# Loading attention's first operands during the recurrence, in the buffer that the projections leave

## What is computed

```python
for window, dil in ((128, 1), (512, 4), (2048, 16)):      # attention, 8 heads x 64
    # positions of equal residue mod dil form a band of window // dil + 1 keys,
    # swept in blocks of 128 queries: own block and the one before
    s = einsum('...qhd,...khd->...hqk', q, k) * ATTN_SCALE + bias
    p = exp(s - max(s)); out, lse = p @ v / sum(p), max(s) + log(sum(p))
# the three outs are weighed by softmax(lse)
S_t = diag(f_t) S_{t-1} + (1 - f_t) i_t^T;  o_t = S_t^T q_t   # recurrence, 4 heads
```

## Time and profile before

| | us |
|---|---|
| median of 3 runs | 1754.37 |
| profiled execution, its own time | 1760.19 |
| its span | 1758.4 |
| TensorE busy | 1570.9 |
| VectorE busy | 806.8 |
| ScalarE busy | 475.8 |
| GpSimd busy | 353.6 |

### The profile page before, as it was taken

One profiled execution on the slowest core, in us unless ns is written; L12 is line 12 of the kernel. 1 busy time (PEld: TensorE's weight loads), 2 busy tenths in 40 slices (PEclk: granted clock), 3 DMA queues, 4 the chain that ended last, 5 costly groups with the idle time before them and its releaser, 6 DMA issues. The chain is left out here.

```text
span 1758.4 us, 26175 instructions
## 1 busy us (share of the span) xinstructions
PE 1570.9 (89%) x9834; PEld 1411.0 (80%) x9834; DVE 806.8 (46%) x2031; ACT 475.8 (27%) x1350; POOL 353.6 (20%) x269
## 2 busy tenths in 40 slices
PE   8999999979899989999799995499989995399987
PEld 7999999966687767777599995498979895277775
DVE  6111200023232142111179883175737574699995
ACT  5111111121001132222201221165646565212210
POOL 1333200001500010000000002538482932011111
PEclk9999999989899989999959997697969798599999
DMA  9999992338748598757201886928592814555541
GB/s 307 350 324 327 338 284 73 127 110 258 213 140 318 181 308 249 271 162 245 88 1 63 259 276 180 257 59 180 144 213 63 169 51 148 216 182 211 212 152 42
DMA packets 180895, 340.67 MB, mean 194 GB/s; under 512 B 16323, under 2 KB 116099, under 8 KB 173443
## 3 DMA queue, kind: packets, MB, share of 16 engines
q1 hardware_dynamic: 147100, 173.77, 31.0%
q10 hardware_dynamic: 21248, 108.93, 19.4%
q0 software_dynamic: 12432, 56.48, 12.1%
HBM read 263.40 MB, written 156.48 MB: 239 GB/s over the span
## 5 line engine op out<-in xcount | busy, mean ns | idle before, releaser
L254 PE MATMUL acc<-xhi,whi 128*128 128x424 f32 (+1 forms) x640 | 227.3, 355 | 8.5 <-DVE xlo L233 8.5
L743 PE MATMUL nacc<-nwhi,nxhi 128*128 128x512 f32 (+1 forms) x544 | 220.2, 405 | 9.2 <-DVE nwlo L492 9.2
L254 PE MATMUL acc<-xlo,whi 128*128 128x424 f32 (+1 forms) x640 | 227.0, 355 | 0.0
L254 PE MATMUL acc<-xhi,wlo 128*128 128x424 f32 (+1 forms) x640 | 226.9, 355 | 0.0
L1320 ACT ACTIVATE spare<-spare 128x256 f32<-128x256 f32 (+1 forms) x384 | 174.1, 454 | 165.0 <-DVE spare L1295 161.9
L743 PE MATMUL nacc<-nwlo,nxhi 128*128 128x512 f32 (+1 forms) x544 | 215.6, 396 | 0.0
L743 PE MATMUL nacc<-nwhi,nxlo 128*128 128x512 f32 (+1 forms) x544 | 215.2, 396 | 0.0
L1252 POOL CAST a_sorted<-a_plain 128x2048 fp32r<-128x2048 f32 x48 | 181.6, 3855 | 154.5 <-PE a_s_ps L1360 128.5
L1295 DVE CUSTOM_DVE_ANT_0 spare<-a_s_ps,a_bias 128x256 f32<-128x256 f32 (+1 forms) x384 | 125.3, 364 | 167.4 <-PE a_s_ps L1360 167.2
L1384 PE MATMUL a_o_ps<-a_v,a_probT 128*128 128x64 f32 x1200 | 170.3, 284 | 20.3 <-DMA a_v<-projN 20.0
L1384 PEld LDWEIGHTS a_o_ps<-a_v,a_probT 128*128 128x128 f32 x1200 | 164.4, 208 | 21.8 <-issue 21.0
(11 more groups left out here) (170 smaller groups left out, 2530.8 us busy)
## 6 DMA issues: line engine op xcount, KB each, us to landing
out_kwin_s<-in_cache_kT ACTq DMA_DIRECT2D x8, 2048.0 KB, 18.3
split_qk<-spare POOLq DMA_DIRECT2D x16, 1024.0 KB, 13.3
spare<-in_xT SPq DMA_DIRECT2D x32, 512.0 KB, 7.6
projN<-nstage SPq DMA_DIRECT2D x32, 512.0 KB, 5.9
qg<-in_cache_kT ACTq DMA_DIRECT2D x8, 2048.0 KB, 10.8
d_vlow<-in_cache_v ACTq DMA_DIRECT2D x8, 2048.0 KB
out_kwin_s<-in_cache_kT ACTq DMA_DIRECT2D x8, 2032.0 KB, 26.1
out_vwin_s<-in_cache_v ACTq DMA_DIRECT2D x8, 2032.0 KB, 16.9
```

The costliest lines, as they stand in the source:

```text
L254: mm = pe.matmul(acc[:, j, 0:n], w[:, u, k], x[:, k, c0:c0 + n], start=(k == 0 and a == 0), stop=(k == KD - 1 and a == 2))
L743: mm = pe.matmul(acc[0:m, n % 2], x[:, u, k, 0:m], w[:, k, g * H:(g + 1) * H], start=(k == 0 and b == 0), stop=(k == KD - 1 and b == 2))
```

## The change

- `spare` lives on the other side of SBUF and only until the projections end. In its room stand, from the start of the recurrence, `plain` of both heads, `ident` and the bias rows of group 0. `stage` and `prob` get buffers of their own, `v` becomes two buffers and so does `bias`.
- POOL issues both `load_pair`s of group 0 in `hgrn_prompt`, right after its memset of `at`; SP issues the identity and `load_bias` of group 0 there, after `load(1)`.
- At the start of attention SP issues `load_values(0)`, the bias of group 1, `load_values(1)`; POOL goes straight to its wait and the sorts.
- `load_pair` loads whole rows: 6 transfers for x = 0 too, in every group. `FRONT` and `front_landed` are gone; TensorE waits for `pair_landed[x]` at the first unit of each head.

```diff
-    def sb(name, shape, dt=F32):
-        return ctx.enter_context(nc.sbuf_tensor(name, shape, dt))
+    def sb(name, shape, dt=F32, side="left"):
+        return ctx.enter_context(nc.sbuf_tensor(name, shape, dt, side=side))
...
+def load_pair(pool, split_qk, plain_x, g, x, landed):
+
+    hs = slice(x * DA, (x + 1) * DA)
+    for n, w, low, half in ((0, 0, 0, 0), (0, 0, 1, 1), (1, 1, 0, 0), (1, 1, 0, 1), (2, 1, 1, 0), (2, 1, 1, 1)):
+        pool.dma_start(plain_x[half * DA:(half + 1) * DA, n], split_qk[w * NG + g, low, hs]).then_inc(landed, 16)
+
+
+def load_bias(sp, rep_p, bias_u, g, landed):
+    L = HA * NC * LB
+    for x in range(2):
+        src = bass.AP(tensor=rep_p.tensor, offset=(2 * g + x) * NC * LB + P - 1, ap=[[L - 1, P], [LB, NC], [1, 2 * P]])
+        sp.dma_start(bias_u[:, x], src).then_inc(landed, 16)
+
+
+def hgrn_prompt(nc, projT, projN, o_b, state_out, first, win, copied, split_qk, rep_p, ident_d, keep):
...
                 load(0)
                 load(1)
+                sp.dma_start(keep["ident"][:], ident_d).then_inc(keep["const"], 16)
+                load_bias(sp, rep_p, keep["bias"][0], 0, keep["bias_landed"][0])
                 for s in range(NSEG):
...
                 nc.gpsimd.memset(at[:], 0.0).then_inc(zeroed, 1)
+                for x in range(2):
+                    load_pair(pool, split_qk, keep["plain"][x], 0, x, keep["pair_landed"][x])
...
-        plain = [sb(f"a_plain{x}", [P, 3, T], F32R) for x in range(2)]
-        ns, np_ = 2 * NBK * 2 * OW, 4 * 2 * 2 * P
-        stage = keep["spare"][:, 0:ns].rearrange("p (w b x e) -> p w b x e", w=2, b=NBK, x=2)
-        prob = keep["spare"][:, ns:ns + np_].rearrange("p (n y k) -> p n y k", n=4, y=2)
-        v = sb("a_v", [P, 2, NC, NBK, P])
-        bias = sb("a_bias", [P, 2, 2, NC, 2 * P])
+        plain, ident, bias = keep["plain"], keep["ident"], keep["bias"]
+        v = [sb("a_v0", [P, NC, NBK, P], side="right"), sb("a_v1", [P, NC, NBK, P])]
+        stage = sb("a_stage", [P, 2, NBK, 2, OW])
+        prob = sb("a_prob", [P, 4, 2, 2 * P])
         probT = sb("a_probT", [P, 3, 4, P])
-        ident = sb("a_ident", [P, P])
+        bias.append(sb("a_bias1", [P, 2, NC, 2 * P]))
         sorted_ = sb("a_sorted", [P, 2, 3, T], F32R)
         s_ps, t_ps, o_ps = ps("a_s_ps", [P, 3, 512]), ps("a_t_ps", [P, 3, 512]), ps("a_o_ps", [P, 2, 512])
...
-        FRONT = 4 * P
-
-        def load_part(pool, w, g, x, c0, c1, landed):
-
-            hs = slice(x * DA, (x + 1) * DA)
-            for n, low, half in ((0, 0, 0), (0, 1, 1)) if w == 0 else ((1, 0, 0), (1, 0, 1), (2, 1, 0), (2, 1, 1)):
-                pool.dma_start(plain[x][half * DA:(half + 1) * DA, n, c0:c1], split_qk[w * NG + g, low, hs, c0:c1]
-                              ).then_inc(landed, 16)
-
...
-                load_bias(0)
-                sp.dma_start(ident[:], ident_d).then_inc(const, 16)
                 load_values(0)
-                load_bias(1)
+                load_bias(sp, rep_p, bias[1], 1, bias_landed[1])
                 load_values(1)
...
-                def load_pair(g, x):
-                    if x == 0:
-                        load_part(pool, 0, g, 0, 0, FRONT, front_landed)
-                        load_part(pool, 1, g, 0, 0, FRONT, front_landed)
-                    for w in range(2):
-                        load_part(pool, w, g, x, 0 if x else FRONT, T, pair_landed[x])
-
                 def sort(g, c, x):
                     d = DILS[c]
                     if c == 1:
-                        if x == 0:
-                            pool.wait_ge(front_landed, 96 * (g + 1))
                         pool.wait_ge(pair_landed[x], 96 * (g + 1))
...
-                load_pair(0, 0)
-                load_pair(0, 1)
...
-                            load_pair(g + 1, x)
+                            load_pair(pool, split_qk, plain[x], g + 1, x, pair_landed[x])
...
-                                pe.wait_ge(pair_landed[1] if x else front_landed, 192 * i + 96 * (u + 1))
-                            if c == 0 and x == 0 and P * (b + 2) == FRONT + 2 * P:
-                                pe.wait_ge(pair_landed[0], 192 * i + 96 * (u + 1))
+                                pe.wait_ge(pair_landed[x], 192 * i + 96 * (u + 1))
...
+        keep = {"ost_free": [sem(f"h_ost_free{u}") for u in range(2)], "state_kept": sem("h_state_kept"), "const": sem("a_const"),
+                "pair_landed": [sem(f"a_pair_landed{x}") for x in range(2)], "bias_landed": [sem(f"a_bias_landed{u}") for u in range(2)]}
+        with ExitStack() as mid:
             with ExitStack() as ctx:
                 sb, _, _ = region(ctx, nc)
-                first["bounds"] = sb("bounds", [P, 4, HB])
-                first["lmask"], first["dmask"] = sb("lmask", [P, len(PLEVELS), CH // 2], I32), sb("dmask", [P, CH], I32)
-                first["ident"], first["qg"] = sb("ident3", [P, P]), sb("qg", [P, 4 * HB * SEG])
-                halves = first["qg"][:].rearrange("p (a u h t) -> p a u h t", a=2, u=2, h=HB)
-                first["q"], first["sg"] = halves[:, 0], halves[:, 1]
-                project_natural(nc, a, projT, projN, o["kwin_p"], o["vwin_p"], o["kwin_s"], o["vwin_s"], rep_p, rep_d, o_b,
-                                attn_s, o["hgrn_s"], spare, w_landed, x_landed, first)
-                hgrn_prompt(nc, projT, projN, o_b, o["hgrn_p"], first, win, copied, keep)
-            attention_prompt(nc, split_qk, projN, rep_p, a["ident"], partials, keep)
+                with ExitStack() as early:
+                    spare = region(early, nc)[0]("spare", [P, 2 * KD * XCOLS], side="right")
+                    project_transposed(nc, a["xT"], a["w_t"], projT, split_qk, win, copied, spare, a["w_n"], w_landed, x_landed)
+                    first["bounds"] = sb("bounds", [P, 4, HB])
+                    first["lmask"], first["dmask"] = sb("lmask", [P, len(PLEVELS), CH // 2], I32), sb("dmask", [P, CH], I32)
+                    first["ident"], first["qg"] = sb("ident3", [P, P]), sb("qg", [P, 4 * HB * SEG])
+                    halves = first["qg"][:].rearrange("p (a u h t) -> p a u h t", a=2, u=2, h=HB)
+                    first["q"], first["sg"] = halves[:, 0], halves[:, 1]
+                    project_natural(nc, a, projT, projN, o["kwin_p"], o["vwin_p"], o["kwin_s"], o["vwin_s"], rep_p, rep_d, o_b,
+                                    attn_s, o["hgrn_s"], spare, w_landed, x_landed, first)
+                right = region(mid, nc)[0]
+                keep["plain"] = [right(f"a_plain{x}", [P, 3, T], F32R, side="right") for x in range(2)]
+                keep["ident"], keep["bias"] = right("a_ident", [P, P], side="right"), [right("a_bias0", [P, 2, NC, 2 * P], side="right")]
+                hgrn_prompt(nc, projT, projN, o_b, o["hgrn_p"], first, win, copied, split_qk, rep_p, a["ident"], keep)
```

More of the change, by code:

```diff
@@ L855, in load_segment @@
     sp.dma_start(q[:, u], projT[8:12, :, t0:t0 + SEG].rearrange("h p t -> p h t")).then_inc(landed[u], 16)
-def hgrn_prompt(nc, projT, projN, o_b, state_out, first, win, copied, keep):
+def load_pair(pool, split_qk, plain_x, g, x, landed):
[8 more added lines that the diff above has]
+def hgrn_prompt(nc, projT, projN, o_b, state_out, first, win, copied, split_qk, rep_p, ident_d, keep):
     NG2 = HB // 2
@@ L1108, in _, with attention_prompt @@
                     read_out(NSEG - 1, c)
-def attention_prompt(nc, split_qk, projN, rep_p, ident_d, partials, keep):
+def attention_prompt(nc, split_qk, projN, rep_p, partials, keep):
     NBK = T // P
@@ L1163, in attention_prompt @@
         stage_free = [sem(f"a_stage_free{w}") for w in range(2)]
-        const, s_done, p_done, p_turn, e_done = (sem(f"a_{n}") for n in ("const", "s_done", "p_done", "p_turn", "e_done"))
+        s_done, p_done, p_turn, e_done = (sem(f"a_{n}") for n in ("s_done", "p_done", "p_turn", "e_done"))
         t_done, pt_done, pv_done, o_out = (sem(f"a_{n}") for n in ("t_done", "pt_done", "pv_done", "o_out"))
-        front_landed, sort_done = sem("a_front_landed"), sem("a_sort_done")
-        pair_landed = [sem(f"a_pair_landed{x}") for x in range(2)]
-        bias_landed = [sem(f"a_bias_landed{u}") for u in range(2)]
+        pair_landed, bias_landed, const = keep["pair_landed"], keep["bias_landed"], keep["const"]
+        sort_done = sem("a_sort_done")
         NLD = 6
-        FRONT = 4 * P
-        def load_part(pool, w, g, x, c0, c1, landed):
-            hs = slice(x * DA, (x + 1) * DA)
-            for n, low, half in ((0, 0, 0), (0, 1, 1)) if w == 0 else ((1, 0, 0), (1, 0, 1), (2, 1, 0), (2, 1, 1)):
-                pool.dma_start(plain[x][half * DA:(half + 1) * DA, n, c0:c1], split_qk[w * NG + g, low, hs, c0:c1]
-                              ).then_inc(landed, 16)
         with nc.Block() as block:
@@ L1183, in _ @@
                 sp.sem_inc(stage_free[1], 16)
[L1185 to L1191, removed]
                 def load_values(g):
@@ L1196, in load_values @@
```

(10 more changed lines are left out.)

2 lines of the change are left out of this document (1 added, 1 removed).

## The result

The changed kernel takes 1727.42 us (median of 4 runs, 1725.64 to 1729.23), against 1756.19 us (4 runs, 1753.92 to 1759.91) for the kernel before on the same chip: ratio 0.983, 95% interval [0.981, 0.986]. It is 28.8 us faster where 69 were forecast, and lies 18 us above the upper end of the range.

The account below looks back on a forecast made before the run. TensorE bounds attention through a 20.0 us wait for values (transfer rate at the start) and 12.4 us of sort waits that halve its clock. 31.9 + 9.2 + 22.2 + 5.7 = 69.0 us off 1754.4 gives 1685.4, said 1686; range 1678 to 1709.

Parts of the forecast that it names:

- Part 1: Start of attention: pair, bias and identity loads move into the recurrence, so the wait for the values ends 31.9 us earlier.
- the case in which the change does not do what it says: Start of attention: SP's slow issuing was its own, values still land near 1134; 1717 us, chance 0.05.
- the slowing weighed there: Recurrence: busy VectorE may lock out GpSimd's descriptor writing; even ten times slower issues, 60 us, would fit the slack.
- Part 2: Unit 40, groups 0 to 2: six issues fewer start sort(2, 1) 3.08 us earlier per group, 9.2 us in all.
- Part 3: Behind unit 40's 1.0 us wait: the clock holds, giving 22.2 us in units 40 to 47 and 5.7 us after.
- The row from the merge: Merge: TensorE waits 1.26 us before each tile's transposes at clock 1.00, taken as evidence that the clock holds.
- The 22.2 us of units 40 to 47: Groups 0 to 2: at full clock these eight units take 8.96 us instead of 16.38, three times.
- the 5.7 behind them: After unit 47: full clock gains 1.0 and 2.3 us at borders of groups 0 and 2, 2.4 at the loop's turn.
- The second case: Units 40 to 47: the clock still falls after 1 us waits, only 41.1 us are left; 1713 us, chance 0.18.
- Part 4: Unit 48: TensorE now waits for the whole next pair, which lands in time with 5 us to spare; costs nothing.
- three of 1 us: Unit 40, groups 0 to 2: TensorE still waits 1.0 us instead of 4.1 in each group.

Follow-up runs that it names:

- experiment 1: Changed kernel with x = 0 pair loads cut into 12 transfers again and the 512-column wait restored, early loads kept; 1725.53 us, ratio 0.982 to the kernel before.
- experiment 8: Kernel before with only SP's order at the start of attention changed: identity, values, then bias of group 0; no early load; 1760.96 us, ratio 1.002.
- experiment 2: Kernel before with only whole-row pair loads (6 transfers for x = 0) and no waits for `front_landed`; 1754.91 us, ratio 0.9987.
- experiment 3: Changed kernel with six identity products before TensorE's wait for the sort at unit 40, in all four groups; 1728.95 us, ratio 0.983 to the kernel before.
- 5: Changed kernel with identity products before unit 40's wait and the x = 1 load held until the c = 1 store has landed; 1716.29 us, ratio 0.977.
- 6: Changed kernel with SP issuing the pair loads of groups 1 to 3, x = 0 ahead of the c = 1 store, x = 1 behind it; 1702.11 us, ratio 0.969.
- experiment 7: Changed kernel without the pair loads of groups 1 to 3, which attend with group 0's queries and keys; 1687.82 us, ratio 0.960 to the kernel before.
- 9: Against the kernel whose later pair loads SP issues: x = 1 for group 2 loaded behind the c = 2 stores; 1698.76 us, ratio 0.967 to the kernel before.
- experiment 4: Changed kernel with POOL holding the x = 1 load until the c = 1 results' store has landed; 1720.59 us, ratio 0.978 to the kernel before.

## Why the prediction was wrong

**Part 1 was right.** 30.9 us instead of 31.9, with the values 1 us later than taken; experiment 1 gives it alone, 31.5 us by its ratio. That the start is bound by transfer rate and not by SP's order is what experiment 8 shows, so the case in which the change does not do what it says is out. The loads were issued in 6.18 us beside a busy VectorE, so the slowing weighed there did not occur. They ended at about 910 instead of 902, still deep in the empty stretch.

**Part 2 was right in its term** (8.8 us instead of 9.2), and worth little in the end: 2.3 us in experiment 2.

**Part 3 is the step that failed:** "I take it that the clock holds." It fell within two units of waits of 1.24, 1.19 and 1.19 us. The 22.2 us of units 40 to 47 became 3.3, and of the 5.7 behind them nothing came: the turn took 1.0 more. The row from the merge did not carry over. The runs agree on it: with 4.2 us of wait (1) and with 1.2 us (the changed kernel, 2) the clock falls, with the wait filled by products (3, 5) or not there (6, 7, 9) units 40 to 47 stay at 1.00. The length of the wait does not decide it alone, though. Of nine waits of 1.16 to 1.25 us at unit 40 (the changed kernel, 2 and 4) eight brought the clock down, and the one in group 1 of experiment 4 did not. At unit 56, the first of x = 1, waits of 3.15 us (5), 1.62 us (6) and 1.22 us (9) brought it down, and waits of 1.30 us (6), 1.27 and 2.35 us (9) did not. What else decides stays open, and neither place had a wait shorter than 1.16 us. So the forecast's rows could not settle the question either way.

The second case, with a chance of 0.18, was the right one on the clock. The section "HAM oscillation — how this bites in real kernels" of the Trainium skill's TensorE: Matmul & The Clock Gate page warns that waits between bursts of matmuls throttle the engine again and again. The traces agree with it for eight of the nine waits at unit 40, which are 1.2 us, and differ for the ninth.

**Part 4 left a resource out.** It asked only whether the next pair lands in time for unit 48, and it does. It did not ask what else must get through while 6.3 MB of loads are under way, with a DMA share of 1.0 to 1.26 from 1160 to 1185. Three things do, and each holds up TensorE once it arrives early enough: the c = 1 store, for which VectorE waits (4 takes that wait away); the operands of x = 1 (5 and 6); and whatever the "issue" gaps at the turn stand for. The first of those gaps is 2.13 us where the loads are over the earlier trace rows and 2.59 in the changed kernel, where they are nearly over; it is 8 to 9 where they are under way (3, 4, 5, 6), 3.2 without them (7) and 4.05 with one put off (9). The likely reading is the fetch of the new turn's instructions, which cross the same DMA engines. The packets of the instruction queues bear it out: in all eleven traces the last packet of queue 8 ahead of the warm-up ends 1.5 to 1.8 us before it (2.5 in experiment 2), and in 3, 4, 5 and 6 another ends about 1.3 us before the warm-up's second part. With the loads out of the way (7) the first such packet starts 0.4 us into the gap, in 6 it starts 4.7 us into it. Since the traces do not say whose instructions a packet carries, that the gap depends on the loads is shown, and that the fetch is what waits is strongly suggested.

The store is why the changed kernel is at 1727 and not at the second case's 1713: set against the profiled run of before the second case gives 1719.1, and 1729.2 were measured. Of the 10.1 between them the borders' waits are 9.3, the merge's 1.4, the turn 1.0 and what parts 1 and 2 fell short 1.4, less the 3.3 that units still at full speed won; 0.3 is left over. It is also why the forecast would have failed with a clock that held: experiment 3 had that clock, and took 1729 us. Only experiment 7, without the loads, reached 1688, two above the number predicted. That is in part luck: it has no wait left at unit 40, where the forecast kept three of 1 us.

A rule of the Trainium skill bears on the first of the three: its DMA: Bandwidth & Descriptors page, section "Queues, rings and completion order", has each DMA engine take turns between its queues one packet at a time. The traffic rows agree in kind: in the same 6 us, with 217 and 216 packets, POOL's queue moved 1.38 MB and SP's 0.11.

## What to carry to other kernels

Before crediting a shorter wait with a faster clock, look for waits of that length in the same stage, and for more than one: a row from another stage said nothing here, and in this stage waits of 1.16 to 2.35 us went both ways. Filling the wait with cheap products or removing its cause held the clock every time. When an engine is made to arrive earlier at a border, list everything that has to cross the DMA engines there (stores that free a buffer, the second half of the operands, the next turn's code), and not only the operand asked for first. Issue a small store that someone waits for ahead of the bulk loads (experiment 4 shows what that gives); one queue for both, in the order in which they are needed, is a way to do it that worked here (6).

## What was not expected of the hardware

- Small-packet stores in SP's queue beside 8 KB rows in POOL's: 12.5 us to landing (median) where 6.9 were seen before, the last of them some 21 us after its issue. In one queue with the loads (6) the same store took 7.8 to 8.0 us.
- The gap at the hardware loop's turn, 2 to 4 us, is 11 to 12 us in two parts when a pair's load is under way.
- The granted clock fell within two units of a wait of only 1.2 us, in a stage of narrow products that had run at 1.00 for the 50 us before; yet it held behind one of 2.35 us in the same stage (9).
- At the turn of the hardware loop packets of the instruction queues move inside TensorE's gap, and the first of them only after 4.7 us while a load is under way (6).
